# Expert blocks: the down products of a block moved, in four parts, between halves of the next block's gate and up products

## The reference

```python
def expert_block(args):
    xb, e = args
    return (jax.nn.silu(xb @ w1[e]) * (xb @ w3[e])) @ w2[e]
...
out = jnp.zeros((T, D), h.dtype).at[tok_s].add((w_s[:, None] * ys[dest]).astype(h.dtype))
```

## Time and profile before

| What | us |
|---|---|
| Median of 3 runs | 1707.37 |
| The profiled execution's own time | 1708.82 |
| Its span, from the first instruction to the last | 1707.0 |
| Mean granted clock of TensorE | 0.987 of full speed |
| TensorE busy (matmuls) | 1603.3, 94% |
| TensorE weight loads busy | 1038.2, 61% |
| DVE, ACT, POOL busy | 675.0, 404.0, 176.6 |
| Bytes moved | 362.38 MB, mean 212 GB/s |

### The profile page before, as it was taken

How to read it: one execution, slowest core, us unless ns; L and a number is a source line. 1 busy time by engine, 2 the same in 40 slices (tenths; PEclk the granted TensorE clock), 3 DMA queues, 4 the chain that set the end, 5 groups by cost and what they waited for, 6 DMA issues and landing times. The chain is left out here.

```text
span 1707.0 us, 37111 instructions
## 1 busy us (share of the span) xinstructions
PE 1603.3 (94%) x15961; PEld 1038.2 (61%) x15961; DVE 675.0 (40%) x1682; ACT 404.0 (24%) x897; POOL 176.6 (10%) x220
## 2 busy tenths in 40 slices
PE   5999999999999999999999999989999999999873
PEld 3444444897787787644444445557777776676652
DVE  4533234323667667776555455572001001000003
ACT  4100000002666667510100002222121211112212
POOL 1205000000101110000000000001111111111100
PEclk9899999999999999999999999999999999999997
DMA  9864331327201007424542172299999999999996
GB/s 345 249 204 132 98 99 54 116 63 222 52 25 45 33 3 242 153 76 130 142 132 83 38 273 84 86 362 361 363 394 395 387 383 398 393 396 406 405 406 260
DMA packets 163745, 362.38 MB, mean 212 GB/s; under 512 B 28631, under 2 KB 111183, under 8 KB 138971
## 3 DMA queue, kind: packets, MB, share of 16 engines
q1 hardware_dynamic: 141456, 316.12, 50.4%
q0 software_dynamic: 12608, 28.01, 6.2%
q10 hardware_dynamic: 9516, 15.85, 2.7%
HBM read 323.48 MB, written 48.50 MB: 218 GB/s over the span
## 5 line engine op out<-in xcount | busy, mean ns | idle before, releaser
L2784 DVE TENSOR_TENSOR sb_m_hT<-psum,sb_m_sg 128x256 f32<-128x256 f32 (+2 forms) x32 | 15.3, 477 | 300.6 <-PE psum L2900 300.6
L2621 ACT ACTIVATE sb_w_o_sb<-psum,sb_rowmod 128x64 f32<-128x64 f32 (+2 forms) x256 | 82.0, 426 | 203.1 <-PE psum L2888 203.1
L868 PE MATMUL psum<-sb_vD,sb_room 128*128 128x512 f32 x240 | 104.6, 592 | 0.0
L2900 PE MATMUL psum<-sb_w_o_sb,sb_front 128*64 128x64 f32 (+2 forms) x2560 | 93.1, 231 | 10.7 <-issue 8.1
L2900 PEld LDWEIGHTS psum<-sb_w_o_sb,sb_front 128*64 128x64 f32 x2560 | 90.4, 138 | 18.3 <-issue 17.2
L1186 ACT ACTIVATE sb_d_probs<-sb_d_probs,sb_d_nmax 128x640 f32<-128x640 f32 (+7 forms) x128 | 92.8, 735 | 12.3 <-DVE sb_d_nmax L1227 11.8
L1782 PE MATMUL psum<-sb_w_o_sb,sb_room 128*128 128x512 f32 x192 | 85.6, 603 | 0.0
L868 PEld LDWEIGHTS psum<-sb_vD,sb_room 128*128 128x128 f32 x240 | 45.6, 190 | 57.4 <-issue 57.4
L1155 PE MATMUL psum<-sb_vS,sb_room 128*64 128x65 f32 x2112 | 79.4, 225 | 0.3 <-ACT sb_room L1173 0.3
L1173 ACT COPY sb_room<-psum 128x512 f32<-128x512 f32 (+1 forms) x108 | 59.5, 550 | 81.4 <-PE psum L1140 81.4
L1140 PE MATMUL psum<-sb_const,sb_d_probs 128*128 128x128 f32 x528 | 75.8, 280 | 1.8 <-ACT sb_front L1186 0.7
(11 more groups left out here) (466 smaller groups left out, 2704.5 us busy)
## 6 DMA issues: line engine op xcount, KB each, us to landing
sb_front<-in_exp_w_dram SPq DMA_DIRECT2D x30, 2048.0 KB, 15.4
sb_mT<-in_exp_w_dram SPq DMA_DIRECT2D x20, 2048.0 KB, 22.3
sb_room<-in_exp_w_dram SPq DMA_DIRECT2D x18, 2048.0 KB
sb_rows<-in_exp_w_dram SPq DMA_DIRECT2D x18, 2048.0 KB, 21.7
sb_w_o_sb<-in_exp_w_dram SPq DMA_DIRECT2D x10, 2048.0 KB, 14.2
sb_g_ada<-in_ada_w_dram SPq DMA_DIRECT2D x16, 1024.0 KB, 5.2
d_qk<-sb_n_b_sel ACTq DMA_DIRECT2D x20, 512.0 KB, 3.3
sb_front<-in_w_in_dram SPq DMA_DIRECT2D x16, 512.0 KB, 5.4
```

Source lines behind the costliest of these rows:

```text
L868: mm = pe.matmul(k.psum[:, bank(g, i), :], w[:, kk, :], x[:, kk, :], start=(kk == 0), stop=(kk == KD // 2 - 1))
L2621: last = act.activation(dst[:, kk, 0:w], src, ACT.Identity, scale=k.rowmod[:, 0, kk:kk + 1], bias=k.rowmod[:, 1, kk:kk + 1])
L2784: tt(hT[:, :, 0:width[b]], hidden_ps(1, width[b]), sg[:, :, 0:width[b]], ALU.mult).then_inc(s_hid, 1)
L2900: mm = pe.matmul(k.psum[part, which, c * w:(c + 1) * w], view[:, kk, first:first + 2 * CAPS - 1:2], x[:, kk, 0:w], start=(kk == 0), stop=( ...
```

## The change

On TensorE, for blocks 1 to 30, the down product of the block before is cut into four parts of four matmuls, one for each chunk c of the hidden rows. The order for block b is now: first half of gate b, down part 0 of b-1, second half of gate b, down part 1, turn of b+1, first half of up b, down part 2, second half of up b, down part 3. Blocks 0 and 31 keep whole gate and up products, and the down products of 30 and 31 stay whole.

SP loads in the order in which the matrices are now first read (`load_order`), POOL's code is as before, and DVE forms the hidden rows of block b+1 ahead of scaling the output of block b. Two slots of the ring change places, so that the loads sent ahead are the same six matrices.

```diff
+def load_order():
+    loads = [(0, 0), (0, 1)]
+    for b in range(1, NE - 1):
+        loads += [(b, 0), (b - 1, 2), (b, 1)]
+    return loads + [(NE - 2, 2), (NE - 1, 0), (NE - 1, 1), (NE - 1, 2)]
...
-AHEAD, FETCHED = 3, 6
+AHEAD, FETCHED = 3, (0, 1, 2, 3, 4, 6)
...
         def _(sp):
...
+            for n, (b, i) in enumerate(loaded):
+                if n in FETCHED:
+                    continue
+                if i == 0:
+                    expert[b] = sp.value_load(be_i[0:1, order[b]:order[b] + 1], min_val=0, max_val=NE - 1)
...
+                if n >= RING:
+                    last, part = loaded[n - RING]
+                    sp.wait_ge((s_gate, s_up, s_y)[part], last + 1)
...
             for b in range(NE):
-                if b >= 1:
-                    hidden(b)
+                if 1 <= b + 1 < LAST:
+                    hidden(b + 1)
+                elif b == LAST:
+                    hidden(LAST)
                 dve.wait_ge(s_y, b + 1)
...
+            def ready(b):
+                if b >= 2:
+                    pe.wait_ge(s_ys, b - 1)
+                if b == 0:
+                    pe.wait_ge(s_idx, 2)
+                if b == 1:
+                    pe.wait_ge(s_be, 1)
+                landed(b, 2)
+                pe.wait_ge(s_hid, b + 1)
+
+            def downs(b, some):
+                for c in some:
+                    mm = down(c, width[b], 4 + 2 * (b % 2), down_w(slot_of(b, 2)))
+                if KE - 1 in some:
+                    mm.then_inc(s_y, 1)
...
             for b in range(NE):
+                mixed = 1 <= b < LAST
...
+                if mixed:
+                    project(0, width[b], xT[b % 2], gate_w(slot_of(b, 0)), some=halves[0])
+                    ready(b - 1)
+                    downs(b - 1, (0,))
+                    project(0, width[b], xT[b % 2], gate_w(slot_of(b, 0)), some=halves[1]).then_inc(s_gate, 1)
+                    downs(b - 1, (1,))
...
+                if mixed:
                     pe.wait_ge(s_g[(b + 1) % 2], gathers(b + 1))
                     turn(xg[(b + 1) % 2], width[b + 1], s_turned)
+                if b >= 1:
+                    pe.wait_ge(s_hid, b)
+                landed(b, 1)
+                if mixed:
+                    project(1, width[b], xT[b % 2], gate_w(slot_of(b, 1)), some=halves[0])
+                    downs(b - 1, (2,))
+                    project(1, width[b], xT[b % 2], gate_w(slot_of(b, 1)), some=halves[1]).then_inc(s_up, 1)
+                    downs(b - 1, (3,))
...
+                if b >= LAST - 1:
+                    ready(b)
+                    downs(b, range(KE))
```

More of the change, by code:

```diff
@@ L1960, in fetch @@
             def fetch(n):
-                e, i = divmod(n, 3)
+                e, i = load_order()[n]
                 w = (k.exp_w1, k.exp_w3, k.exp_w2)[i]
-                sp.dma_start(*expert_matrix(w, slice(e, e + 1), slots[n], i == 2)).then_inc(k.s_first[n], 16)
+                sp.dma_start(*expert_matrix(w, slice(e, e + 1), slots[n], i == 2)).then_inc(k.s_first[FETCHED.index(n)], 16)
             fetch(0)
@@ L1985, in _ @@
             sp.wait_ge(s_done, done(NPAIR - 1, M3))
-            fetch(5)
+            fetch(6)
             sp.wait_ge(s_sum, 16 * (NT - 1))
@@ L2466, in stage_moe @@
         width = [capacity(r) for r in order]
-        slot_of = lambda b, i: (3 * b + i) % RING
-        loads = lambda b, i: 16 * ((3 * b + i) // RING + (0 if (3 * b + i) % RING < FETCHED else 1))
+        loaded = load_order()
+        place = {load: n for n, load in enumerate(loaded)}
+        slot_of = lambda b, i: place[b, i] % RING
+        loads = lambda b, i: 16 * (place[b, i] // RING + (0 if place[b, i] % RING in FETCHED else 1))
         LAST = NE - 1
-        free = [slot_of(LAST - 2, 0), slot_of(LAST - 2, 1), slot_of(LAST - 2, 2), slot_of(LAST - 3, 2)]
+        free = [slot_of(LAST - 2, 0), slot_of(LAST - 2, 1), slot_of(LAST - 1, 0), slot_of(LAST - 3, 2)]
         ya = [ring[free[t // 4]][:, (t % 4) * D:(t % 4 + 1) * D] for t in range(NT)]
@@ L2490, in _ @@
         def _(sp):
[L2491 to L2504, removed]
+            expert = {}
+            for n, (b, i) in enumerate(loaded):
[3 more added lines that the diff above has]
+                    expert[b] = sp.value_load(be_i[0:1, order[b]:order[b] + 1], min_val=0, max_val=NE - 1)
+                if n == SPARE:
+                    sp.wait_ge(s_onehots, 2)
+                    sp.wait_ge(s_slots, 1)
+                if n >= RING:
+                    last, part = loaded[n - RING]
+                    sp.wait_ge((s_gate, s_up, s_y)[part], last + 1)
+                w = (k.exp_w1, k.exp_w3, k.exp_w2)[i]
+                sp.dma_start(*expert_matrix(w, bass.ds(expert[b], 1), ring[slot_of(b, i)], i == 2)).then_inc(s_w[slot_of(b, i)], 16)
             sp.wait_ge(s_y, LAST - 1)
@@ L2890, in turn, with project @@
                 tr.then_inc(done, 1)
-            def project(which, w, x, view, rest=None):
-                for c in range(KE):
+            def project(which, w, x, view, rest=None, some=range(KE)):
+                for c in some:
                     for kk in range(KD):
@@ L2911, in landed @@
             def landed(b, i):
-                if b < KNOWN:
-                    pe.wait_ge(k.s_first[3 * b + i], 16)
+                if place[b, i] in FETCHED:
+                    pe.wait_ge(k.s_first[FETCHED.index(place[b, i])], 16)
                 else:
@@ L2922, in _ @@
+            halves = (range(KE // 2), range(KE // 2, KE))
             for b in range(NE):
+                mixed = 1 <= b < LAST
                 pe.wait_ge(s_xT, b + 2 if b else 1)
-                if b == 0:
-                    pe.wait_ge(k.s_first[0], 16)
-                else:
[L2927 to L2934, removed]
@@ L2935, in _ @@
-                project(1, width[b], xT[b % 2], gate_w(slot_of(b, 1))).then_inc(s_up, 1)
-                if 1 <= b and b + 1 < NE:
+                if b >= 1:
+                    pe.wait_ge(s_silu, b)
+                landed(b, 0)
+                if mixed:
[4 more added lines that the diff above has]
+                    downs(b - 1, (1,))
+                else:
+                    project(0, width[b], xT[b % 2], gate_w(slot_of(b, 0)), 0 if b else 2).then_inc(s_gate, 1)
@@ L2937, in _ @@
+                if mixed:
                     pe.wait_ge(s_g[(b + 1) % 2], gathers(b + 1))
                     turn(xg[(b + 1) % 2], width[b + 1], s_turned)
+                if b >= 1:
+                    pe.wait_ge(s_hid, b)
[5 more added lines that the diff above has]
+                    downs(b - 1, (3,))
+                else:
+                    project(1, width[b], xT[b % 2], gate_w(slot_of(b, 1))).then_inc(s_up, 1)
@@ L2983, in build @@
         k.s_dil4 = k.sem("dilated_set4_stored")
-        k.s_first = [k.sem(f"first_expert{i}") for i in range(FETCHED)]
+        k.s_first = [k.sem(f"first_expert{i}") for i in range(len(FETCHED))]
         k.s_kT, k.s_brow_out, k.s_tables = k.sem("cmp_rows"), k.sem("bias_rows"), k.sem("bias_tables")
@@ L3018, in build @@
             ring = [k.front[:, 4 * D * i:4 * D * (i + 1)] for i in range(AHEAD)] + [
-                flat(mT[:, 0:4, :]), flat(w_o[:, 0:4, :]), flat(mT[:, 4:8, :]),
-                room[:, 0:4 * D], room[:, 4 * D:8 * D], flat(rows[:, 4:8, :]), flat(rows[:, 0:4, :])]
-            stage_out(k, mT, g1row, w_o, rows, chosen, s_wo, room, ring[0:FETCHED])
+                flat(mT[:, 0:4, :]), flat(w_o[:, 0:4, :]), room[:, 0:4 * D], flat(mT[:, 4:8, :]),
+                room[:, 4 * D:8 * D], flat(rows[:, 4:8, :]), flat(rows[:, 0:4, :])]
+            stage_out(k, mT, g1row, w_o, rows, chosen, s_wo, room, ring)
             columns = [w_o[:, 5 + i, :].rearrange("p (k t) -> p k t", k=KD) for i in range(2)]
```

## The result

The changed kernel takes 1720.78 us, the median of 6 runs (1718.49 to 1723.69), beside 1708.17 us (1705.77 to 1710.55, 6 runs) for the kernel before. The ratio is 1.0066, 95% interval 1.0053 to 1.0079: slower by 0.66%, 12.6 us by the medians and 11.3 by the ratio. Forecast were +11 us and 1718.4.

What follows compares the result with a forecast made beforehand. The 16 DMA engines were taken to bound the expert stage from 1217 us on. 8.5 us for the first loads and 2.5 for the tail, on 1707.4, gave 1718.4 us; range 1707 to 1725, the forecast's own 1713 to 1725.

Steps and rivals of the forecast that it cites:

- The bound: Expert stage from 1217 us: the 16 DMA engines, at share 1.02, set the end, not TensorE's order of products.
- The first loads: Blocks 0 to 3: slots freed later, so loads 12 to 19 go out later and DMA engines idle; 8.5 us lost.
- The switches: Eight changes between products in an interleaved block, costed at nothing; at most 1.5 us a block, kept in the range.
- No harm later: After the early blocks, bunched slot releases cost nothing, since the transfer backlog grows by 1.7 us a pair of blocks.
- The rate: 389 GB/s from 1217 and 404 from 1514 at share 1.02: taken as full, without the 10% reserve 435 GB/s would imply.
- DVE's wait: The down product's wait for DVE's hidden rows, which interleaving would cover: only 1.9 us in 7 places.
- The stops called issue: 27.9 us of TensorE stops inside gate and up products, without a semaphore wait in the code; the change leaves them.
- The queues: On POOL, gathers are issued about 20 us before the turn needs them, so their delay behind an add is hidden.
- The tail: After the last load: down 30 waits bare for DVE, block 30's add waits for block 29's; 2.5 us, bounds 1 and 5.
- Catch-up: Rival: transfers have 11 us of reserve from 1217 on and make up the loss; 1707 to 1710 us, chance 0.14.
- TensorE gains: Rival: TensorE sets the pace and a third of its issue stops go; about 1699 us, chance 0.08.
- Late gathers: Rival: gathers behind queued loads land late in 6 wide blocks, +20 us, 1738; chance 0.10 together with dearer switches.

Runs made afterwards that it cites:

- range(1, 30): The changed kernel with block 30 back in the old order; ratio 1.0052 to the kernel before, median 1718.74 us.
- range(14, 30): The changed kernel interleaving only in blocks 14 to 29, all others in the old order; ratio 0.9997 to the kernel before, median 1708.29 us.

## Why the prediction was right

**The bound.** Right, and shown from three sides: 10.2 us more for TensorE in block 14 cost 0.9, half the chunks less in nine up products (14.1 us less busy) gained nothing that can be told, and the DMA share stands at 1.02 in both stretches between 1217 and 1640.

**The first loads.** Right in place; the closeness in size is partly luck. 8.5 were forecast, 10.0 read from the share. By place 2.1, 5.5 and 2.0 were forecast and 4.5 (0.7 of it there before), 5.8 and 1.4 read. Each release was 1.7 to 3.4 us later than forecast, for two reasons that the bounds covered. The switches, costed at nothing, take 0.13 us for a quarter and 0.11 for a half, so about 1.0 us in a block of 80 or 112 rows; where the down product is of 64 rows a quarter takes 0.86 us, no more than a quarter of 3.5. And gate 1's first half took 3.77 us, not 2.25: after its wait for ACT TensorE was granted half its clock (see below). That belongs to this execution and not to the change, and so does part of the 10.0: the two other traces with the same code up to block 4 give 6.5 and 11.6, and the forecast lies between. Neither reason matters after block 3.

**No harm later.** Right: both stretches from 1217 to 1640 stand at 1.02, though each block of 80 or 112 rows takes TensorE a microsecond more. From block 14 on the interleaving costs nothing that can be told (-2.1 to +1.0 us).

**The rate.** The two rates of before at the same share of 1.02 were read rightly. POOL's transfers (the software queue) took 14.8% of the engines' time in the slower stretch and 10.9% in the other. Single stretches differ more: 344 GB/s from 1190 to 1195 and 425 from 1185 to 1190, both at 1.01. So GB/s at a full share tells the mix of transfers and not a reserve.

**DVE's wait.** Right: 0.5 us of it went, and gained nothing.

**The stops called issue.** Wrong: "the change leaves them". Of the 27.9 us in gate and up products 5.4 were left, and TensorE waited for down matrices instead. The sum did not use these stops, so the forecast did not suffer. Why they went was not tried.

**The queues.** Right: no turn waits for a gather. The gathers landed a median of 10 to 12 us after issue (12.1 for the 80- and 112-row blocks), against the 20 us of lead; the adds 10.

**The tail.** Right in number, by luck in one step: 2.5 forecast, 2.9 in the trace, 2.4 and 3.1 from the pairs with and without block 30. The chain is in the trace as forecast, down 30 bare behind DVE (0.72 us) and two adds in a row (8.85 us). With the 3.2 us, and less the 10.0 of the first loads, the add of block 30 goes out at 1673.5, forecast 1673.5. But from there the prediction's own 8.1 us for an add and its issue of 1.55 give reads at 1683.2, 7.4 us late, and it said 4 without a reason. Measured were 4.3, since the last add took 5.0 us and not 8.1. Why it was shorter was not tried. That the two adds are what the tail costs is argued and not shown: adds in a row stand at the end of `range(1, 30)` and `range(14, 30)` too.

**The rivals.** *Catch-up*: out. The rate from 1217 to 1514 is 388 GB/s, with 10 us to make up and TensorE busier than before. The Trainium skill (Perfetto Trace Analysis, Roofline) gives about 435 GB/s for a lone core's 16 engines. The measurement decides: that was no reserve here, and with the gathers' and adds' packets among the weights', a share of 1.02 at 388 is full. Whether weights alone could go faster over a long stretch, no run here shows. *TensorE gains*: out. Its premise came in part, since the stops inside the products fell by 22.5 us and the wait for DVE by 0.5, and still the time rose: TensorE then waited for the matrices. *Late gathers*: out.

## What to carry to other kernels

Where the transfers never pause, reordering the compute was worth nothing here, and it cost what it held a ring slot longer while no transfers were queued. Before interleaving, list which product frees the slot of each of the first loads, and compare the time at which each goes out; the price is the idle time of the DMA engines until they are full, once, whatever happens in later blocks. The same list says what helps: short blocks first (0.2 to 3.8 us here). Interleaving does no harm only from where the queue is deeper than the delay, and here it gained nothing there either. And before a stop called issue is taken for the engine's own, look in the code for a semaphore wait at its place.

## What the hardware showed that was not expected

In the changed kernel TensorE was busy 5.4 of the 6 us up to 1166, then idle for 2.67 us behind ACT, up to 1168.5. For the start of gate 1 it was granted half its clock (1.2 instead of 2.4 GHz): 0.50 and 0.67 in these stretches.

```profile
1168.50:1170.00 1.50, 1.46 (x22) 1.47 (x24) 0.69 (x3) 0.00 (x0) 0.00 (x0) 0.50 1.02 421
1170.00:1172.00 2.00, 2.00 (x44) 2.00 (x43) 0.00 (x0) 0.00 (x0) 0.00 (x0) 0.67 0.99 408
```

It made 64 matmuls take 3.77 us, where the next 64 took 2.44. So a wait that looks like 2.7 us cost 4.0 in this execution. It doesn't always. In the kernel with less work on TensorE, whose code is the same up to there, the same wait left the clock whole:

```profile
1168.91 2.44 PE L2912 MATMUL psum<-sb_w_o_sb,sb_front 128*64 128x80 f32 x64 [2.67 <-ACT sb_w_o_sb L2631]
```

Eight of the traces have such a wait, of 2.7 to 2.9 us, ahead of the first interleaved gate. In three of them the half gate behind it took its usual time, 2.44 or 3.29 us. In the other five it took 1.3 to 2.9 us more, 6.20 instead of 3.29 at the most. What decides between the two was not tried. In `range(14, 30)` the wait and the slow half gate (4.54 us instead of 2.44) both stand in the trace, and the time is that of the kernel before.
